# GpSimd makes the low halves of the Q and V weight pieces, on a semaphore of its own

## What is computed

```python
for l in range(DEPTH):                              # 2 layers
    h = rmsnorm(x, norm1_g[l])
    q, k, v, qi, ki, wi, pool_in, conv_in = split_columns(h @ w_in[l])
    # dsa_attention: an indexer scores the keys of each query, the best 128 are kept
    score = einsum('bqhs,bqh->bqs', relu(qi . ki), wi)
    _, sel = lax.top_k(score, 128)
    y_a = softmax(q . k[sel]) @ v[sel]
    x = x + concat([y_a, y_b, y_c]) @ w_out[l]      # y_b pooling, y_c conformer convolution
    h2 = rmsnorm(x, norm2_g[l])
    # hier_moe: 16 experts (4 groups of 4), each D=1024 -> 512 (gate and up) -> 1024 (down)
    x = x + hier_moe(h2, ...)
return rmsnorm(x, final_g)
```

## Time and profile before

| | us |
|---|---|
| median of 3 runs | 1256.43 (1256.05 to 1260.15) |
| the profiled execution | 1255.91 |
| its span, first to last instruction | 1254.1 |
| mean granted TensorE clock | 0.963 |
| PE busy | 1135.0 (91%) |
| DVE busy | 1010.9 (81%) |
| ACT busy | 734.8 (59%) |
| POOL busy | 115.8 (9%) |

### The profile page before, as it was taken

One profiled execution on the slowest core, in us unless ns is written; L12 is line 12 of the kernel. 1 busy time (PEld: TensorE's weight loads), 2 busy tenths in 40 slices (PEclk: granted clock), 3 DMA queues, 4 the chain that ended last, 5 costly groups with the idle time before them and its releaser, 6 DMA issues. The chain is left out here.

```text
span 1254.1 us, 18376 instructions
## 1 busy us (share of the span) xinstructions
PE 1135.0 (91%) x5700; PEld 901.3 (72%) x5700; DVE 1010.9 (81%) x1561; ACT 734.8 (59%) x1050; POOL 115.8 (9%) x165
## 2 busy tenths in 40 slices
PE   5999978998999999999489999789989999999980
PEld 5866854786788888888378577458677888888870
DVE  5898986346799999999559899752658999999975
ACT  5234148332788888888332342682427888888862
POOL 4100000001011011110400000000000011111103
PEclk9999979999999999999699999799999999999995
DMA  9722201229799999998454122002379999999935
GB/s 295 274 73 70 99 19 34 68 68 330 270 394 391 393 392 393 392 392 303 165 191 120 66 84 68 34 29 90 139 280 331 393 392 393 392 392 393 392 139 219
DMA packets 146436, 293.14 MB, mean 234 GB/s; under 512 B 17248, under 2 KB 19344, under 8 KB 146368
## 3 DMA queue, kind: packets, MB, share of 16 engines
q1 hardware_dynamic: 130176, 237.63, 52.8%
q0 software_dynamic: 16192, 54.69, 11.8%
HBM read 265.50 MB, written 26.74 MB: 233 GB/s over the span
## 5 line engine op out<-in xcount | busy, mean ns | idle before, releaser
L355 PE MATMUL ps<-w_hi,a_hi 128*128 128x512 f32 x960 | 380.8, 397 | 11.4 <-DVE arena L1342 6.7
L343 ACT ACTIVATE w_hi<-raw 128x1024 fp32r<-128x1024 f32 (+1 forms) x256 | 268.2, 1053 | 208.6 <-PE ps L357 200.4
L357 PE MATMUL ps<-w_hi,a_lo 128*128 128x512 f32 x960 | 375.3, 391 | 0.0
L356 PE MATMUL ps<-w_lo,a_hi 128*128 128x512 f32 x960 | 374.9, 391 | 0.0
L347 DVE TENSOR_TENSOR w_lo<-raw,w_hi 128x1024 fp32r<-128x1024 f32 (+1 forms) x256 | 303.3, 1210 | 80.3 <-ACT w_hi L343 70.9
L347 DVE TENSOR_TENSOR w_lo<-arena,w_hi 128x1024 fp32r<-128x1024 f32 x192 | 227.8, 1221 | 8.9
L343 ACT ACTIVATE w_hi<-arena 128x1024 fp32r<-128x1024 f32 x192 | 204.3, 1064 | 43.7 <-PE ps L357 40.9
L355 PEld LDWEIGHTS ps<-w_hi,a_hi 128*128 128x128 f32 x960 | 181.1, 189 | 48.5 <-DVE a_lo L1333 7.1
L357 PEld LDWEIGHTS ps<-w_hi,a_lo 128*128 128x128 f32 x960 | 180.8, 188 | 38.1
L356 PEld LDWEIGHTS ps<-w_lo,a_hi 128*128 128x128 f32 x960 | 181.3, 189 | 35.7
L355 PE MATMUL ps<-a_hi,w_hi 128*128 128x512 f32 (+1 forms) x304 | 122.0, 401 | 5.1 <-DVE a_lo L1176 5.1
(11 more groups left out here) (207 smaller groups left out, 1157.1 us busy)
## 6 DMA issues: line engine op xcount, KB each, us to landing
arena<-in_w_down SPq DMA_DIRECT2D x144, 256.0 KB, 9.4
raw<-in_w_gate SPq DMA_DIRECT2D x136, 256.0 KB, 7.9
raw<-in_w_up SPq DMA_DIRECT2D x136, 256.0 KB, 10.3
arena<-in_w_gate SPq DMA_DIRECT2D x120, 256.0 KB, 8.3
arena<-in_w_up SPq DMA_DIRECT2D x120, 256.0 KB, 8.6
raw<-in_w_down SPq DMA_DIRECT2D x112, 256.0 KB, 9.3
raw<-in_w_in SPq DMA_DIRECT2D x80, 256.0 KB, 5.1
y_rows<-arena POOLq DMA_DIRECT2D x48, 256.0 KB, 5.8
```

The costliest lines, as they stand in the source:

```text
L343: nc.scalar.activation(split_slot(w_hi, n, w), place(S, i, n, w), ACT.Copy).then_inc(S.w_hi_set, 1)
L355: nc.tensor.matmul(o, lh, rh, start=start, stop=False)
L356: nc.tensor.matmul(o, lh, rl, start=False, stop=False)
L357: return nc.tensor.matmul(o, ll, rh, start=False, stop=stop)
```

## The change

DVE's eight `lo` in the top-k rounds of each layer are gone. GpSimd makes the same eight subtractions (pieces 16 to 23, `QV`) from its own queue, behind the zero stores of layer 0 and behind the load of `pw` in layer 1, and raises a semaphore of its own, `qv_lo_set`. Since `w_lo_set` no longer counts those eight, a function `lo_set` works out for each piece which semaphore and which value tells that its low half is made; `load`, `use` and the branch for overflow tiles ask it. Two semaphores for small inputs, `rout_in` and `pbd_in`, become one, `tiny_in`, and the two that waited for them now wait for all ten of these DMAs.

```diff
@@ -49,6 +49,7 @@
+QV = range(PIECES_GROUP * G_Q, PIECES_GROUP * (G_V + 1))
...
+        qv_lo_set = sem("qv_lo_set")
...
+        def lo_set(S, i, n):
+
+            if S is not main:
+                return S.w_lo_set, n + 1
+            l, m = divmod(n, PIECES_L)
+            if i is None and m in QV:
+                return qv_lo_set, len(QV) * l + QV.index(m) + 1
+            return w_lo_set, cnt(i, RING_E, n + 1 - len(QV) * (l + (m >= QV.stop)))
+
         def load(sp, S, i, n, sources, w=1024):
...
             if last is not None and (i is not None or last >= 0):
-                sp.wait_ge(S.w_lo_set, cnt(i, RING_E, last + 1))
+                sp.wait_ge(*lo_set(S, i, last))
...
         def use(pe, S, i, n):
-            pe.wait_ge(S.w_lo_set, cnt(i, RING_E, n + 1))
+            pe.wait_ge(*lo_set(S, i, n))
...
                 with sp.If(extra > 0):
-                    sp.wait_ge(main.w_lo_set, n)
+                    sp.wait_ge(*lo_set(main, None, n - 1))
...
+                for m in QV:
+                    n = l * PIECES_L + m
+                    pool.wait_ge(w_hi_set, n + 1)
+                    g.tensor_tensor(split_slot(w_lo, n, 1024), place(main, None, n), split_slot(w_hi, n, 1024).bitcast(F32),
+                                    ALU.subtract).then_inc(qv_lo_set, 1)
...
-                            pe.wait_ge(pbd_in, 16 * 2 * DEPTH)
+                            pe.wait_ge(tiny_in, 16 * (2 + 4 * DEPTH))
...
-                    ve.wait_ge(rout_in, 16 * (2 + 2 * DEPTH))
+                    ve.wait_ge(tiny_in, 16 * (2 + 4 * DEPTH))
...
                 for r in range(ROUNDS):
-                    if r < 12 and r % 3 != 2:
-                        lo(ve, main, None, n0 + 16 + r // 3 * 2 + r % 3)
                     topk_round(l, r)
```

More of the change, by code:

```diff
@@ L209, in trunk @@
         head = sb("head", [P, 2, 16])[:]
-        cst_in, chan_in, rout_in, pbd_in, x_in, pads = sem("cst_in"), sem("chan_in"), sem("rout_in"), sem("pbd_in"), [sem(f"x_in{tt}") for tt in range(TT)], sem("pads")
+        cst_in, chan_in, tiny_in, x_in, pads = sem("cst_in"), sem("chan_in"), sem("tiny_in"), [sem(f"x_in{tt}") for tt in range(TT)], sem("pads")
         chan_t, chan_set, rw_split = sem("chan_t"), sem("chan_set"), sem("rw_split")
@@ L478, in _ @@
             g.memset(arena[0:CHUNK, A_MB0 + CHUNK:A_MB0 + P], MASKED).then_inc(pads, 1)
-            pool.dma_start(rb[:, :, 0:NG], t["rg_b"].partition_broadcast(P)).then_inc(rout_in, 16)
-            pool.dma_start(rb[:, :, NG:20], t["re_b"].partition_broadcast(P)).then_inc(rout_in, 16)
+            pool.dma_start(rb[:, :, 0:NG], t["rg_b"].partition_broadcast(P)).then_inc(tiny_in, 16)
+            pool.dma_start(rb[:, :, NG:20], t["re_b"].partition_broadcast(P)).then_inc(tiny_in, 16)
             for l in range(DEPTH):
                 pool.dma_start(rw[:, l, :, 0:NG], t["rg_w"][l].rearrange("(c p) n -> p c n", p=P),
-                               allow_slow_non_contiguous=True).then_inc(rout_in, 16)
+                               allow_slow_non_contiguous=True).then_inc(tiny_in, 16)
                 pool.dma_start(rw[:, l, :, NG:20], t["re_w"][l].rearrange("(c p) n -> p c n", p=P),
-                               allow_slow_non_contiguous=True).then_inc(rout_in, 16)
+                               allow_slow_non_contiguous=True).then_inc(tiny_in, 16)
                 for h in range(2):
                     pool.dma_start(pbd[h * 64:(h + 1) * 64, l, :, h * 64:(h + 1) * 64],
-                                   t["pool_w"][l, h::2].rearrange("g c d -> c g d")).then_inc(pbd_in, 16)
+                                   t["pool_w"][l, h::2].rearrange("g c d -> c g d")).then_inc(tiny_in, 16)
             for l in range(DEPTH):
```

## The result

The changed kernel takes 1275.89 us (median of 4 runs, 1275.13 to 1276.98); the kernel before, run beside it, 1257.8 (4 runs). The ratio is 1.0135, with a 95% interval of 1.011 to 1.0161, so 18.1 us are lost. The prediction had 1260.1 and a range up to 1265.0: it gave "slower" 0.45 against 0.43 for "same", so the sign is only just its own; the mechanism (the loads that are held back) was right, the size was not. The profiled execution of the changed kernel has a span of 1274.3 us, 20.2 above the 1254.1 of before.

The account below looks back on a forecast made before the run. In the experts TensorE was taken to set the pace, with the DMA engines having nothing to spare. The profiled 1255.9 us - 4.3 + 8.0 gave 1259.6, and 0.5 more for the median 1260.1; range 1252.0 to 1265.0.

Parts of the forecast that it names:

- part 1: Top-k rounds: VectorE drops eight subtractions a layer, unit 0 comes 2.14 us earlier, 7.0 become waiting; sum -4.3 us.
- part 3: Experts' loop: 20 of 24 loads a round wait for a count 8 too high; 4.0 us a layer, sum +8.0; 82%.
- rival (b): Top-k rounds: VectorE and GpSimd block each other, so the gain goes or reverses; 1264 us and more, 4%.
- the 2.14 stay: Attention, behind unit 0: the chain is as before, so the 2.14 us won there are kept.
- Part 2: Top-k rounds: GpSimd's subtraction takes 2.4 us, keeps up to 5.44 us a piece, and costs TensorE zero.
- The lateness of the loads: Experts: loads land 7.9 us late, 1.6 more from the queue's pause, and stay 9.5 us late to the end.
- The slack: End of the experts: 4.1 us of load lead plus 1.4 of ScalarE's running ahead, 5.5 us to absorb late loads.
- the last group, 218 to 223: Experts' last six loads: no stores between, 8.0 us against TensorE's 8.8, so no worse than the group before.
- The upper bound of 6.6 a layer: Experts: loads late by the full 10.5 us and 1.6 on top, 12.1, cost TensorE 6.6 us a layer.
- (a): Experts: the lead of landed loads hides the late loads entirely, leaving only the -4.3 us; 1252.1 us, 12%.
- (c): Top-k rounds: VectorE's gain stays out and TensorE waits on GpSimd, needing over 5.44 us a subtraction; 1290 at 7 us, 2%.
- The signs that the prediction named: Profile after: VectorE idle 6 to 7 us before unit 0, else (b); ScalarE waiting for DMAs from about the eighth expert.

Follow-up runs that it names:

- mended: The changed kernel with the 8 always subtracted in the hardware loop, GpSimd's subtractions kept: 1258.51 us, ratio 0.9997 to the kernel before.
- hold 8: The kernel before, with only the loop's loads that follow a slot's piece below 24 waiting for a count 8 higher: 1277.64 us, ratio 1.0143.
- hold 4: The kernel before, with only the same loop loads waiting for a count 4 higher: 1266.5 us, ratio 1.0061.
- the runs of 4, 8 and 12: The kernel before, with only the same loop loads waiting for counts 4, 8 or 12 higher: 1266.5, 1277.64 and 1289.76 us.
- a hold of 2: The kernel before, with only the same loop loads waiting for a count 2 higher: 1262.17 us, ratio 1.0013 (0.9999 to 1.0028).

## Why the prediction was wrong, step by step

The prediction's sum was -4.3 for the gain and +8.0 for the hold, 3.7 us; measured were 18.1. The gain came to nothing (mended), and the hold alone cost 19.0 (hold 8). So some 4 of the missing 14.4 us belong to part 1 and the others to part 3.

**Part 1, VectorE's gain: right in kind, a sixth too large, and then lost.** I had 2.14 us a layer at unit 0, and 7.0 us turning into VectorE's wait for TensorE. Unit 0 gained 1.8, and there was no wait. The term that failed stands under rival (b), "five waits of up to 2.4 us mostly disappear in the slack": I had named the taps and taken no price for them. It was four waits of 1.8, 7.3 us, which is the whole of the slack and 0.3 more. The second half, "the 2.14 stay", failed too: the earlier trace rows showed a clock of 0.71 in 163 to 174, and I took the chain behind unit 0 as a constant. It is not one: TensorE's clock sets its length, and mended measured no gain (from 1.9 us won to 1.1 lost) where 4.3 were forecast (with 1.8 for 2.14, 3.6).

**Part 2, GpSimd: right.** 2.4 us a subtraction was forecast from twice VectorE's, 2.40 measured, no wait of TensorE. The Trainium skill's table ("GPSIMD Engine Reference", section 3.1) has 4497 ns for 2048 numbers; the estimate of 2.3 that I had made from it is 0.1 us off.

**Part 3, the hold: the mechanism right, the size less than half.** That 20 of 24 loads wait 8 pieces too long, that piece 76 is the first and goes out some 10.5 us late (12.1, of which 1.5 were late already), that the queue runs dry and the loss isn't made up: all of it is in the trace. The cost was 4.0 us a layer; it is 7.4 in the experts of the changed kernel, and 9.5 by the median of hold 8 (19.0 / 2), whose trace has 8.4 and 7.6 in the experts. Two terms were short. *The lateness of the loads*, 9.5 forecast, is 10.5 to 10.8 by the bytes that weren't moved. *The slack*, 5.5 forecast, is about 3: the step that failed is "the last group, 218 to 223, is no worse, since six loads with no stores between them take 6 x 1.34 = 8.0 us". There were stores and the gains' load between them, and it took 10.0. The traces show both steps: in the changed kernel, beyond what it was late ahead of the hold, TensorE is 5.9 us late at piece 212, where the forecast had 4.0 (mostly the lateness of the loads), and 7.4 at piece 218, where it had 4.0 still (the last group). With hold 4 it is 0.0 and then 2.5. I had read the margin of the last but one group from a row and argued that of the last. The upper bound of 6.6 a layer rested on the same 5.5 us of slack, so the range of the forecast was too narrow from the same step. The rest up to 9.5 lies outside the experts and is not settled: single traces show it as stretches of low clock behind them, and mended has those too.

**The rivals.** (a), the hold is hidden, is out: the runs of 4, 8 and 12 cost 7.9 to 31 us. (b) as the prediction put it, VectorE standing still in all rounds, is out, MAX8 kept its 1.47 us; its cost for the taps alone was real and made the difference between a wait of some 7 us before unit 0 and none. (c) is out by the 3 us that GpSimd waits for ScalarE between two subtractions.

**The signs that the prediction named** would have told it: VectorE has no wait before its first L1490, so "it was (b)" (the taps), and ScalarE's high halves wait for DMAs from piece 140 on (0.9 us there, 2.5 at 146), the tenth expert, near the "eighth" of the prediction. But its own sum did not go with that sign. The loads land a piece in 1.57 us and TensorE uses one in 1.474, so a wait that has begun grows by 0.096 us a piece: 4.0 us at piece 212 mean a first wait 42 pieces earlier, at 170, and a first wait at 140 means 6.9 us at 212 and 8.0 at the end (measured, 5.9 and 7.4). Asked for the onset as well as for the end, the sum would have shown that one of the two was wrong.

## What to carry to other kernels

A load that is held back costs, in a stretch where the DMA engines are at their limit, what they don't move while their queue is short or dry, less the slack of the *last* group of loads (with the holds of 8 and 12, 1 to 2 us more than that), and this slack is to be read from the last group's own landing row, with all that GpSimd moves in between. When a second engine takes over work, look at which instructions of the first have two inputs in SBUF: 0.74 us became 2.57. And a chain that runs through TensorE while its clock is at half is not a constant: what was won ahead of it can be eaten or doubled, so it is worth first keeping TensorE busy in its short idle gaps (8 us here, with 15 idle matmuls a layer) and then counting gains.

## What the runs showed of the hardware that I had not expected

- Fifteen to twenty idle matmuls of 128x128 a layer, in gaps of 0.9 to 2.7 us, took 8 to 10 us off a kernel of 1259 us (ratios 0.9915, 0.9937 and 0.9917 in three runs of two kernels). In the first, the granted clock was 1.00 in 169 to 175 and 179 to 188 us, where it had been 0.50.
- A two-input VectorE instruction that starts 0.4 us behind a GpSimd subtraction is not slowed by a share but waits until about the end of that one: 2.57 in place of 0.74 us, against a subtraction of 2.40, and GpSimd's own time doesn't change. No trace has a tap that starts first.
- The time of a hold is close to a straight line in the number of pieces, 7.9, 19.0 and 31.2 us for 4, 8 and 12, and bytes are missing from the first two on: a queue that isn't dry but holds only a few loads already moves less (with a hold of 2, 356 in place of 393 GB/s in 340 to 376, 166 in its lowest us, 352 to 353; with a hold of 4 it is dry, 24 GB/s from 351 to 354).
